# The bias of the first expert layer: four matrix products against a copy by ScalarE of a row spread by GpSimd

## The reference, cut to what matters

```python
logits = (ht @ router_w + router_b).astype(jnp.float32)
top_val, top_idx = lax.top_k(logits, TOP_K)
gates = jax.nn.softmax(top_val, axis=-1)
...
def expert_block(args):
    idx, e = args
    u = clamped_swiglu(h_pad[idx] @ w1[e] + b1[e])
    return u @ w2[e] + b2[e]
```

## Time and profile before

| | us |
|---|---|
| median of three runs | 1928.5 |
| lowest and highest of them | 1926.17, 1931.32 |
| span of the profiled execution | 1938.0 |
| TensorE busy in that span | 1867.0 (96%) |
| VectorE busy | 1620.9 (84%) |
| ScalarE busy | 1144.5 (59%) |
| GpSimd busy | 323.8 (17%) |
| DRAM traffic over the span | 525.11 MB, 271 GB/s |

### The profile page before, as it was taken

The page is one execution under the profiler, slowest core; times in us unless marked ns, Lnnn a source line. Parts: engine busy times, 40 slices in busy tenths (PEclk is TensorE's granted clock), DMA queues, the critical chain, the costliest instruction groups (busy, mean ns, idle before and its releaser), DMA issues.

```text
span 1938.0 us, 27277 instructions
## 1 busy us (share of the span) xinstructions
PE 1867.0 (96%) x9408; PEld 1520.5 (78%) x9408; DVE 1620.9 (84%) x1752; ACT 1144.5 (59%) x1146; POOL 323.8 (17%) x336
## 2 busy tenths in 40 slices
PE   7999999999999998999999999999999999999997
PEld 6877777866777877888888888888888888888884
DVE  6877677944567577899999999999999999999996
ACT  4423344235563322577777777777777777777773
POOL 2101110020362510611111111111111111111110
PEclk9999999999997987999999999999999999999998
DMA  8545544041001233999999999999999999999994
GB/s 232 173 140 187 166 148 177 22 120 55 1 18 39 89 112 146 312 347 397 391 397 398 389 397 393 390 391 387 393 393 386 394 382 391 398 386 394 388 367 151
DMA packets 176817, 525.11 MB, mean 271 GB/s; under 512 B 30754, under 2 KB 48242, under 8 KB 176754
## 3 DMA queue, kind: packets, MB, share of 16 engines
q1 hardware_dynamic: 152722, 457.48, 62.2%
q0 software_dynamic: 21952, 66.78, 11.9%
q10 hardware_dynamic: 2080, 0.01, 0.1%
HBM read 499.08 MB, written 25.15 MB: 270 GB/s over the span
## 4 chain that ended last, share of the span: by engine, by line
PE 59%; DVE 2%; issue 0%; POOLq 0%; POOL 0%; DVEq 0%
PE banks L3614 54%; PE banks L3602 3%; PE banks L3608 1%; PE banks L3682 0%; DVE expert_weights L3962 0%; DVE x_tokens L3958 0%; DVE weights_lo L3753 0%; PE banks L3703 0%; DVE x_tokens L3969 0%; DVE x_tokens L3841 0%; PE banks L3740 0%; PE banks L3673 0%; DVE rows_lo L3783 0%; DVE member L3821 0%; DVE route_work L3863 0%
## 5 line engine op out<-in xcount | busy, mean ns | idle before, releaser
L3753 DVE TENSOR_TENSOR weights_lo<-expert_weights,weights_hi 128x2048 fp32r<-128x2048 f32 x384 | 876.9, 2289 | 65.3 <-ACT weights_hi L4000 62.3
L4000 ACT ACTIVATE weights_hi<-expert_weights 128x2048 fp32r<-128x2048 f32 x384 | 738.7, 1926 | 264.4 <-PE banks L3614 252.2
L3614 PE MATMUL banks<-weights_hi,rows_hi 128*128 128x512 f32 x1024 | 319.2, 393 | 0.0
L3614 PE MATMUL banks<-weights_hi,rows_lo 128*128 128x512 f32 x1024 | 315.5, 389 | 0.0
L3614 PE MATMUL banks<-weights_lo,rows_hi 128*128 128x512 f32 x1024 | 273.8, 389 | 0.0
L3614 PEld LDWEIGHTS banks<-weights_hi,rows_hi 128*128 128x128 f32 x1024 | 189.8, 188 | 44.9 <-issue 7.3
L3614 PEld LDWEIGHTS banks<-weights_hi,rows_lo 128*128 128x128 f32 x1024 | 192.3, 188 | 40.5
L3614 PEld LDWEIGHTS banks<-weights_lo,rows_hi 128*128 128x128 f32 x1024 | 192.3, 188 | 39.9
L3614 PE MATMUL banks<-weights_hi,u_hi 128*128 128x512 f32 x512 | 161.0, 396 | 0.0
L3614 PE MATMUL banks<-weights_hi,u_lo 128*128 128x512 f32 x512 | 157.9, 390 | 0.0
L3614 PE MATMUL banks<-weights_lo,u_hi 128*128 128x512 f32 x512 | 136.9, 389 | 0.0
(11 more groups left out here) (620 smaller groups left out, 2696.6 us busy)
## 6 DMA issues: line engine op xcount, KB each, us to landing
expert_weights<-in_exp_w SPq DMA_DIRECT2D x384, 1024.0 KB, 10.5
enter_rows<-in_ada_w POOLq DMA_DIRECT2D x24, 1024.0 KB, 6.5
w_in_landing<-in_w_in SPq DMA_DIRECT2D x16, 384.0 KB, 3.4
second_landing<-in_w_in SPq DMA_DIRECT2D x12, 512.0 KB, 3.7
x_tokens<-in_x SPq DMA_DIRECT2D x8, 512.0 KB, 7.2
w_in_landing<-in_w_in SPq DMA_DIRECT2D x8, 512.0 KB, 3.6
rwkv_room<-in_w_o SPq DMA_DIRECT2D x8, 512.0 KB, 6.4
w_in_landing<-in_w_in SPq DMA_DIRECT2D x12, 256.0 KB, 5.1
```

Of the source, the lines that this page charges most:

```text
L3614: last = nc.tensor.matmul(c.banks[:, bank + n, :], left[:, 2 * q + kk, :], right[:, q, kk * FF + n * 512:kk * FF + (n + 1) * 512], start=s ...
L3753: nc.vector.tensor_tensor(w_lo[:, ch % SPLIT, :], c.raw[:, ch % RAW if place is None else place, :], w_hi[:, ch % SPLIT, :], ALU.subtract) ...
L4000: nc.scalar.activation(w_hi[:, ch % SPLIT, :], c.raw[:, ch % RAW if place is None else place, :], ACT.Copy).then_inc(hi_ready.sem, 1)
```

## The change

Three things take the place of the four products. SyncE fetches the bias of an expert as one float32 row of 2048 numbers onto one partition. GpSimd spreads it with `partition_broadcast` over all 128 partitions of `b1all` (two free tiles of `x_tokens`, so that this tensor's name appears in rows). ScalarE's new `seed(i, half)` copies 1024 columns of it into two result banks. TensorE then only adds: its four opening products are gone, and in their place the accumulation state of banks 0 to 3 is set once by `open_banks`, four bf16 products of zeros. The wait of TensorE for the bias row, `lin_ready` and `silu_ready` becomes a wait for `seeded`, once for each half.

In the first mixer VectorE no longer splits the bias in three: three casts and two subtractions fall away, and the add of 1 stays. The counts of the router move from bank 1 to bank 6. `no_pairs` moves into `last_gates_T` to make room.

```diff
                 def split_b1():
                     dve.wait_ge(b1_in.sem, 16)
-                    c.dve(dve, v.tensor_scalar(b1[:, 1::2], b1[:, 1::2], 1.0, None, ALU.add))
-                    for i in range(3):
-                        last = v.tensor_copy(b1_three[:, i, :], b1)
-                        if i < 2:
-                            c.dve(dve, last)
-                            c.dve(dve, v.tensor_tensor(b1, b1, b1_three[:, i, :], ALU.subtract))
-                    last.then_inc(b1_ready.sem, 1)
+                    v.tensor_scalar(b1[:, 1::2], b1[:, 1::2], 1.0, None, ALU.add).then_inc(b1_ready.sem, 1)
...
-        b1row = sb("bias_1_rows", [P, FF // 2], BF16)
-        ones = sb("ones_bf", [P, P], BF16)
+        b1row = sb("bias_1_row", [1, 2 * FF])
+        b1all = c.x[:, 2:4, :].rearrange("p a n -> p (a n)")
...
                 def bias_1(e):
-                    for g in range(4):
-                        sp.dma_start(b1row[32 * g:32 * g + 3, :], bias_rows[:, bass.ds(e, 1), g * 512:(g + 1) * 512].rearrange(
-                            "a o n -> (a o) n")).then_inc(b1_in.sem, 16)
-
-                def first_layer(i, e, s0):
+                    sp.dma_start(b1row[:], bias_rows[bass.ds(e, 1), :]).then_inc(b1_in.sem, 16)
+
+                def first_layer(i, e, s0, after):
                     for k in range(8):
                         if k == 4:
 
-                            sp.wait_ge(b1_used.sem, i)
-                            bias_1(e)
+                            sp.wait_ge(b1_spread.sem, i + 1)
+                            bias_1(after)
...
+                def spread_bias(i):
+
+                    pool.wait_ge(b1_in.sem, i * 16 + 16)
+                    if not (isinstance(i, int) and i == 0):
+                        pool.wait_ge(seeded.sem, i * 2)
+                    pool.sem_inc(fetches.sem, 1)
+                    nc.gpsimd.partition_broadcast(b1all, b1row[:]).then_inc(b1_spread.sem, 1)
+
+                pool.wait_ge(c.sums_stored.sem, 16 * TT)
+                spread_bias(0)
                 pool.wait_ge(no_pairs_in.sem, 16)
                 pool.wait_ge(slots_ready.sem, 1)
                 for t in range(TT):
+                    if t == 1:
+                        spread_bias(1)
                     for k in range(TOPK):
                         nc.gpsimd.indirect_dma_start(table, bass.IndirectOffsetOnAxis(slots[:, t, k:k + 1], 0),
                                                      pairs[:, t, k, :], None).then_inc(slots_in.sem, 16)
+                spread_bias(2)
...
                     fetch(i + 1)
                     add_rows(i - 2)
+                    spread_bias(i + 1)
                     pool.wait_ge(y_added.sem, i * 16 - 16)
                     fetch_pair(i - 1)
...
-                def first_layer(i, s0, later):
+                def first_layer(i, s0):
 
                     pe.wait_ge(x_hi_in.sem, 1 + i)
                     pe.wait_ge(x_lo_in.sem, 1 + i)
-                    pe.wait_ge(b1_in.sem, 64 + i * 64)
-                    if later:
-                        pe.wait_ge(lin_ready.sem, i * 2)
-                        pe.wait_ge(silu_ready.sem, i * 2)
-                    bias().then_inc(b1_used.sem, 1)
                     for half in range(2):
+                        pe.wait_ge(seeded.sem, i * 2 + half + 1)
                         chunks(2 * half, x_hi, x_lo, s0 + 4 * half)
...
+                def seed(i, half):
+
+                    act.wait_ge(b1_spread.sem, i + 1)
+                    if not (isinstance(i, int) and i == 0):
+                        act.wait_ge(silu_ready.sem, i * 2 - 1 + half)
+                    nc.scalar.activation(c.banks[:, 2 * half:2 * half + 2, :].rearrange("p b n -> p (b n)"),
+                                         b1all[:, half * FF:(half + 1) * FF], ACT.Copy).then_inc(seeded.sem, 1)
...
                     silu(i, 0, True)
-                    for k in range(8, 12):
+                    high(8, s0 + 8, landed(8, i - 1), True)
+                    seed(i + 1, 0)
+                    for k in range(9, 12):
                         high(k, s0 + k, landed(k, i - 1), True)
                     silu(i, 1, True)
                     high_rows(i + 1)
+                    seed(i + 1, 1)
```

82 lines of the change are left out of this document (50 added, 32 removed).

## The result

The changed kernel takes 1955.95 us (median of 4 runs, 1955.48 to 1960.03), the kernel before 1929.89 us in the same comparison (4 runs, 1926.17 to 1931.32). The ratio is 1.0128, with a 95% interval of 1.0108 to 1.0149: slower by 1.3%, 26 us. The forecast was 1920.0 us, the range 1917 to 1932: wrong, and on the wrong side. The profiled execution of after has a span of 1954.7 us and belongs to its series; that of before (span 1938.0) is 8 us longer than the median of its runs. So the two profiles lie only 16.7 us apart, and the medians 26.1.

The account below looks back on a forecast made before the run. TensorE was taken to bound the kernel, with VectorE and the DMA engines right behind. -10.7 (products) + 1.0 (DMA engines) + 1.2 (start) = -8.5 us, from 1928.5 to 1920.0 us; range 1917 to 1932.

Parts of the forecast that it names:

- The products' saving: In the expert loop, dropping 32 groups of four bias products saves TensorE 10.7 us, making its step 34.64 us.
- The bias row is 8 KB in one DMA instead of 12 KB in four, which is nothing beside 12 MB.: In each expert step, the new row's DMA was taken to add nothing; DMA engines overall were charged 1 us, 0 to 5.
- the recovery of 0.41 us a step: Weight chunks' landing falls from 12.8 to 9.5 us in 8 steps, so the DMA engines can do 34.56 us a step.
- The rival of a DMA cap: In the loop, DMA engines manage no better than 34.97 us a step, so only the lead is gained: 1924.5 us; chance 0.15.
- The broadcast's length: GpSimd's broadcast to 128x2048 in each step takes 2.1 us, range 1.8 to 4.2.
- The rival of the slow broadcast: GpSimd's broadcast costs as an addition, 4.2 us or more, making VectorE the bound: 1977 us, slower; chance 0.11.
- So up to a broadcast of about 2.3 us the loop is still TensorE's.: In each step, VectorE needs 34.6 us with the broadcast against TensorE's 34.64; the lead covers another 0.17: no cost.
- The stop: VectorE's `low`s, with two SBUF inputs, stand still for the broadcast's whole length, 2.1 us a step.
- a lead of 5.2 us: VectorE finishes chunk 4's low part at about 1138.5 and TensorE wants it at 1143.7, so delays up to 5.2 us are covered.
- Both signs that the prediction had named against itself: Forecast wrong if TensorE idles until `weights_lo` (VectorE bounds) or ScalarE idles until weight DMAs in late steps (DMA engines bound).
- The seeds: ScalarE's two 128x1024 copies a step take 1.01 us each, bringing it to 28.0 of 34.64 us; cost nothing.
- The start of the experts: The first broadcast stops VectorE's router work by up to 2.1 us; charged 1.2 us, between 0 and 2.4.

Follow-up runs that it names:

- g2: The changed kernel without the loop's broadcast (most blocks lack true bias), the loop's bias row DMA cut from 8 KB to 4 bytes; 1930.21 us, ratio 0.9987.
- g1: The kernel before without TensorE's four bias products, nothing added in their place, bias DMAs kept; 1925.76 us, ratio 0.9972.
- e1: The changed kernel with the loop's broadcast replaced by a GpSimd memset of one column, seeds kept (most blocks lack true bias); 1945.32 us, ratio 1.0079.
- h2: The kernel before without its four bias products, its four bias DMAs cut from 1 KB to 4 bytes a row; 1918.34 us, ratio 0.9924.
- h1: e4 with the bias row fetched as 16 pieces of 512 B, still to one partition; 1946.47 us, ratio 1.007.
- k4: e1 with the loop's 8 KB bias row laid over 16 partitions, 512 B each; 1934.44 us, ratio 1.0007.
- e4: The changed kernel with the broadcast moved ahead of the add of rows, beside VectorE's work that reads PSUM; 1946.32 us, ratio 1.0067.
- e2: The changed kernel with the loop's broadcast replaced by a full GpSimd memset of 128x2048, which reads nothing; 1951.46 us, ratio 1.0083.
- e3: The kernel before, bias products kept, plus one broadcast a step to tiles that nothing reads; 1939.39 us, ratio 1.0039.
- g3: e1 plus four products of zeros ahead of the first layer, meant to give TensorE its old length; 1971.36 us, ratio 1.0203.
- h4: h1 with the identity made by three DMAs, other masks behind GpSimd's first DMAs, VectorE's wait for the identity removed; 1951.88 us, ratio 1.0097.

## Why the prediction was wrong

*The products' saving.* "-10.7 ... and the new step of TensorE is 34.64 us": right in kind for TensorE, and too small: it runs a step in 34.5 us in g2, 14.2 us less in the stretch. But taken alone it gives 0.5 us in the stretch of g1's profile (6 us in its median), since the weights do not follow.

*"The bias row is 8 KB in one DMA instead of 12 KB in four, which is nothing beside 12 MB."* This step failed first. The row costs 12.6 us in the stretch (e1 against g2), the old four 12.3 (g1 against h2). I took the recovery of 0.41 us a step from the landing times as the DMA engines' limit, 34.56 us a step. The runs show 34.9 with a row (e1 and g1, stretch over 31.5 steps) and 34.5 without (g2). The one sentence on bytes kept me from asking where they land. Charged 1 us, at most 5. The rival of a DMA cap had the right mechanism (TensorE gains only its lead), but ended at 1924.5, since it had nothing else that costs.

The Trainium skill, DMA: Bandwidth & Descriptors, section "Why a DMA increments its semaphore by 16 and not by 1", says that a DMA issued as these are runs on the largest number of engines, up to 16, that divides the slowest dimension above 1 of both patterns, and that each of them adds its own 1 to the semaphore when its data has landed, while the rest is added at once. By this rule a dimension of 16 has all 16. The trace agrees: 16 late updates for h1 and k4, one for the row in one piece. But it is not the number of engines that costs: h1 has all 16 and still lies 10.7 us above g2 (e4 lies 12.4 above it), and k4 1.8. What is left between h1 and k4 is the single partition at the receiving end, and the gaps between the pieces in DRAM, which no run separates from it.

*The broadcast's length.* 2.1 us taken, 2.30 measured, in the range. The rival of the slow broadcast leaned on a wrong reading: not "every two-input operation of GpSimd" ran at 1.05 us for 128x512. The one of the earlier trace rows took 1.71, and the trace of before has groups from 1.04 to 1.73.

*"So up to a broadcast of about 2.3 us the loop is still TensorE's."* The stop was right in kind (e2) and in size (1.95 us for three `low`s), and e3 shows it hidden at a step of 34.97. It still cost 11.9 us in after (against e1). What failed is that I added up VectorE's need and compared it with the step, as if order did not matter. The stop falls on the `low`s ahead of `lin`; ScalarE's waits for `lin` grow from 54.8 us (e1) to 143.5, and its `high`s stand behind `silu`. I had claimed a lead of 5.2 us and spent the same lead three times, on ScalarE's seeds, on VectorE and on the DMA engines. Both signs that the prediction had named against itself came: TensorE waited for `low`s (12.9 us), and ScalarE for the weights (78.1 us).

*The seeds.* 1.01 to 1.04 us each, as taken, and nothing in the loop where neither a stop nor a heavy row takes the cover (g2). In the tail they do cost. ScalarE of g2 behind its last first-layer product starts (1872.8):

```profile
1881.22 0.60 ACT L4023 ACTIVATE silu<-banks 128x512 f32<-128x512 f32 x1 [0.36 <-DVE lin L3775]
1881.71 1.02 ACT L4036 ACTIVATE rows_hi<-banks 128x1024 fp32r<-128x1024 f32 x1
1882.62 1.04 ACT L4030 ACTIVATE banks<-x_tokens 128x1024 f32<-128x1024 f32 x1
1883.56 5.52 ACT L4016 ACTIVATE weights_hi<-expert_weights 128x2048 fp32r<-128x2048 f32 x3
```

and of h2, which waits for its weights as much but has no seeds (1862.8):

```profile
1868.13 0.60 ACT L4008 ACTIVATE silu<-banks 128x512 f32<-128x512 f32 x1 [0.42 <-DVE lin L3760]
1868.63 1.02 ACT L4013 ACTIVATE rows_hi<-banks 128x1024 fp32r<-128x1024 f32 x1
1869.53 3.74 ACT L4001 ACTIVATE weights_hi<-expert_weights 128x2048 fp32r<-128x2048 f32 x2
```

The last `high`s begin 10.8 us behind in g2, 6.7 in h2, and the tails are 57.0 and 52.4. With TensorE as the bound and the seeds there it is 52.4 too (g3). The rows show a seed of 1.04 us behind `rows_hi` and another at 1872.74; the other 3.1 us of the lag are there at `silu` already. All kernels without seeds have a tail of 52.4 or 52.5, also where the weights are late (g1, h2), and all with seeds have 56.8 to 59.5 but the one that TensorE bounds. So I put the 4.4 us of after to the seeds on a ScalarE without cover; that is argued, since a seed left out there was not tried. The prediction had no term for the end.

*The start of the experts.* +1.2 taken, +1.5 measured. Part of it is the stop that I expected (start, us; the second operation takes 0.29 in before):

```profile
776.44 0.29 DVE L3869 TENSOR_TENSOR over_capacity<-over_capacity,ids_f 128x128 f32<-128x128 f32 x1
776.76 2.25 DVE L3870 SCALAR_TENSOR_TENSOR rank<-over_capacity,rank 128x128 f32<-128x128 f32 x1
```

but the broadcast stood there by accident: the gap ahead of it had held it for 10.9 us.

*The loading of GpSimd's code.* No term at all. 7 us of the 26 are lost in the first 16 us of a program whose mixers were not touched: 6.9 at the DMA of zeros, 7.3 in the median of e3. The profiles of before and after don't show them at the experts, where `ids_i` stands 0.5 us apart, since that of before ran 8 us above its median.

*The sum as it should have been:* stretch -14.2 (before to g2: products and every row gone) + 12.6 (g2 to e1: row) + 11.9 (e1 to after: stop) = +10.3. That is the measured one by construction, since each term is the step from one kernel to the next; what the stop costs in a loop without the row was not tried. Start of the experts +1.5; tail +4.4; start of the program +7.0. Together +23.2 of 26.1. The other 2.9 lie ahead of the experts, where two profiles of one kernel differ by 3 us, and stay open. So does why g1 gained 6 us in its median and 0.8 in its profile.

*Would a better version have been there?* Not with this row. Moving the broadcast (e4) gives 12 of the 26 us back, and the most that spreading the row's landing could add is 10.8 (e1 less k4), which would end some 3 us above before. The loading and the tail stay. k4's way can't be joined to a broadcast that reads one partition.

## What to carry to other kernels

Before taking work off the bounding engine, ask what the runner-up does without its imbalances: 8 KB that all land on one partition cost 0.40 us a step (12.6 over 31.5 steps), in which the loop brings some 140 KB of evenly spread weights (12 MB in 34.5 us). Such a cost was hidden only as long as TensorE was slower. A lead can be spent once: list who draws on it, in the order of each engine's queue, not as sums per step. The first use of an instruction of a kind that the program had not used can cost somewhere else entirely, so compare the first microseconds of the two traces too.

## What the runs showed of the hardware

- GpSimd stood idle, by my reading for the loading of its code, 10.8 us ahead of the first mask and 10.9 us ahead of the first broadcast (10.3 in e1), where neither gap stands in a program without a broadcast. The Trainium skill, GPSIMD Engine Reference, section "Instruction dispatch", gives about 6 us from the `MODIFY_POOL_CONFIG` to the first new instruction, less what it waits for events; here it is 9.8 (766.9 to 776.7), and the row had landed by 766.8.
- A broadcast of 2048 fp32 from one partition to 128 took 2.30 us, a memset of the same size 2.47.
- Four bf16 products of 3 rows and 512 columns took 0.39 us together on partitions 0, 32, 64 and 96, and 0.60 us for two on partition 0.
- A DMA of 64 KB issued at 2.05 us, behind the first loads, landed after 10.5 us (h4).
- 8 KB a step to one partition cost the loop 12.6 us in one piece on one engine (e1) and 10.7 in 16 pieces on 16 (h1); 8 KB to 16 partitions on 16 engines cost 1.8 (k4).
- One broadcast beside two-input `low`s stopped VectorE for 1.95 us (after); a memset of the same size did not (e2), nor did a broadcast beside operations that read PSUM (e4).
